# Mamba outer outputs in the inner outputs' bank, last states turned after the loop, and every low weight on VectorE

## The reference

```python
for l in range(2):
    h = h + 0.5 * swiglu(rms_norm(h, norm_ffn1[l]), ...)      # 1024 -> 2*2816 -> 1024
    u = rms_norm(h, norm_mix[l])
    m = mixer_ab(u) if l == 0 else mixer_c(u)                 # Mamba-2 + GLA, or HGRN2
    h = h + m
    h = h + 0.5 * swiglu(rms_norm(h, norm_ffn2[l]), ...)
y = rms_norm(h, norm_final)
```

```python
xdt = xb * dt
y = einsum(C B^T * decay, xdt)  +  (C h) * exp(cum)  +  D * x     # inner + outer + skip
h_new = h * exp(cum[-1]) + einsum(B, exp(cum[-1] - cum), xdt)      # the state, and at the end an output
y = rms_norm(y * silu(z))
```

## Time and profile before

| | us |
|---|---|
| median of 3 runs | 2534.32 (2531.28 to 2534.85) |
| the profiled execution | 2535.39 |
| its span | 2533.7 |
| TensorE busy | 2439.3 (96%) |
| VectorE, ScalarE, GpSimd busy | 1138.3, 988.4, 680.7 |
| mean granted TensorE clock | 0.984 of 2.4 GHz |

### The profile page before, as it was taken

The page is one execution under the profiler, slowest core; times in us unless marked ns, Lnnn a source line. Parts: engine busy times, 40 slices in busy tenths (PEclk is TensorE's granted clock), DMA queues, the critical chain, the costliest instruction groups (busy, mean ns, idle before and its releaser), DMA issues.

```text
span 2533.7 us, 53953 instructions
## 1 busy us (share of the span) xinstructions
PE 2439.3 (96%) x21434; PEld 2401.3 (95%) x21434; DVE 1138.3 (45%) x1730; ACT 988.4 (39%) x1416; POOL 680.7 (27%) x292
## 2 busy tenths in 40 slices
PE   7999999888899999999999999999999988999998
PEld 7999999887899999999999999999999987999998
DVE  3330335777566653321344330335788854330334
ACT  4331224556345444321223331223777734331222
POOL 3443443000000003443443443443000002443442
PEclk9999999899999999999999999999999998999999
DMA  4332233232322223232332232332222222232231
GB/s 120 89 103 74 83 97 83 70 97 68 99 81 64 67 74 87 83 108 68 90 99 75 84 108 67 91 95 80 64 65 71 62 64 64 87 104 74 84 96 56
DMA packets 395808, 208.80 MB, mean 82 GB/s; under 512 B 9791, under 2 KB 391862, under 8 KB 395670
## 3 DMA queue, kind: packets, MB, share of 16 engines
q1 hardware_dynamic: 390094, 203.09, 27.9%
q10 hardware_dynamic: 5576, 3.77, 0.5%
HBM read 201.39 MB, written 5.45 MB: 82 GB/s over the span
## 4 chain that ended last, share of the span: by engine, by line
PE 85%; DVE 7%; ACT 2%; DVEq 2%; issue 1%; ACTq 1%; POOL 0%; DMA 0%; SPq 0%; POOLq 0%
PE PD L1865 67%; PE PD L1892 12%; PE PM L2205 1%; DVE wlo L1137 1%; PE PM L2215 1%; DVE CV L1292 1%; ACTq L978 1%; PE PM L2238 1%; ACT whi L521 1%; DVEq L1610 1%; POOL wlo L466 0%; DVE c_xl L1608 0%; PE PM L2199 0%; PE PM L2183 0%; PE PM L2064 0%
## 5 line engine op out<-in xcount | busy, mean ns | idle before, releaser
L466 POOL TENSOR_TENSOR wlo<-raw,whi 128x1024 fp32r<-128x1024 f32 (+2 forms) x244 | 668.8, 2741 | 1551.3 <-ACT whi L521 1538.6
L521 ACT ACTIVATE whi<-raw 128x1024 fp32r<-128x1024 f32 (+4 forms) x348 | 381.5, 1096 | 1147.3 <-PE PD L1865 1025.8
L1865 PE MATMUL PD<-XH,whi 128*128 128x272 f32 x3008 | 624.4, 289 | 5.9 <-POOL wlo L466 2.9
L1865 PE MATMUL PD<-XH,wlo 128*128 128x272 f32 x3008 | 621.8, 288 | 0.0
L1865 PE MATMUL PD<-XL,whi 128*128 128x272 f32 x3008 | 621.3, 288 | 0.0
L1865 PEld LDWEIGHTS PD<-XH,whi 128*128 128x128 f32 x3008 | 473.1, 188 | 8.0 <-issue 4.0
L1865 PEld LDWEIGHTS PD<-XL,whi 128*128 128x128 f32 x3008 | 473.5, 189 | 0.0
L1865 PEld LDWEIGHTS PD<-XH,wlo 128*128 128x128 f32 x3008 | 470.8, 189 | 0.0
L1865 PE MATMUL PD<-AL,whi 128*128 128x272 f32 x1408 | 291.3, 288 | 0.0
L1865 PE MATMUL PD<-AH,whi 128*128 128x272 f32 x1408 | 291.1, 288 | 0.0
L1865 PE MATMUL PD<-AH,wlo 128*128 128x272 f32 x1408 | 290.2, 287 | 0.0
(11 more groups left out here) (402 smaller groups left out, 2616.7 us busy)
## 6 DMA issues: line engine op xcount, KB each, us to landing
raw<-in_ffn_w_gu SPq DMA_DIRECT2D x176, 512.0 KB, 3.8
raw<-in_ffn_w_down SPq DMA_DIRECT2D x32, 768.0 KB, 4.8
raw<-in_ab_w_in SPq DMA_DIRECT2D x44, 512.0 KB, 4.0
raw<-in_ffn_w_down SPq DMA_DIRECT2D x32, 640.0 KB, 4.5
raw<-in_c_w_in SPq DMA_DIRECT2D x32, 512.0 KB, 4.1
LM<-cum_rows SPq DMA_DIRECT2D x8, 512.0 KB, 4.9
raw<-in_ab_w_out SPq DMA_DIRECT2D x16, 256.0 KB, 2.8
raw<-in_ab_w_out SPq DMA_DIRECT2D x8, 512.0 KB, 4.0
```

The lines of the kernel that those rows point to most:

```text
L466: pool.tensor_tensor(wlo[u % 2][:, 0:k, :], raw[u % 4][:, 0:k, :], whi[u % 2][:, 0:k, :].bitcast(F), ALU.subtract).then_inc(S["lo_ready"], 1)
L521: A(whi[ps % 2][:, 0:k, :], raw[ps % 4][:, 0:k, :], ACT.Copy).then_inc(S["hi_ready"], 1)
L1865: last = mm(PD[:, 2 * (ps % 2) + s, 0:HT], wt[ps % 2][:, r, :], x[:, r, s * HT:(s + 1) * HT], start=(p == 0 and q == 0), stop=(p == 2 and ...
```

## The change

- **Outer outputs.** `outputs(j)` writes them to bank 1, columns 32 to 479, beside the 32 inner columns of the sample; `y_read` of pair j-1 is now waited for there, and `output(j)` on DVE reads them there. `turn(j)` waits for x alone.
- **Last states.** The chain of DVE leaves them untransposed in HIO and HSIO; PE turns all eight of a kind at once, into banks 2 and 3: `state_turn(0)` behind `outputs(7)`, `state_turn(1)` behind unit 6 of `ab_outy0`. ACT copies them back with two copies each. SS has two tiles less.
- **Means.** They go to banks 0 and 1. `mean(0)` stands ahead of `products(5)` instead of `turn(5)`, ACT's `y_rstd(0)` behind `decay(5)`, and `outputs(5)` waits for it. The wait for `y_read` of the last pair moves from ahead of unit 5 to behind the first half of unit 6, and the last rows' copy (CLST) behind `y_rstd(1)`.
- **DVE's order at m = 7.** The four `y_low` go ahead of `gate_row(7)`.
- **Low weights.** POOL makes units 0 and 1 only; DVE makes all others, each (`lo_ahead`) behind the evacuation of the unit two before it, inside the loops, which now go over four units with the last round written out.

```diff
@@ POOL
-            def lo(u, i, k):
...
+            for u in range(2):
+                pool.wait_ge(S["hi_ready"], u + 1)
+                pool.tensor_tensor(wlo[u][:, 0:KT, :], raw[u][:, 0:KT, :], whi[u][:, 0:KT, :].bitcast(F),
+                                   ALU.subtract).then_inc(S["lo_ready"], 1)
+            pool.wait_ge(S["unit_done"], plan["ab_heads"][0] + CREDIT)
+            states_out(pool)
+            scan_consts(GM)
+            pool.wait_ge(S["rs_ready"], 5)
+            scan_consts(CM)
@@ ACT
-            def state_rows(j):
-                act.wait_ge(S["st_turned"], j + 1)
-                A(HIO[:, j, :], PM[:, 1, P:2 * P], ACT.Copy)
-                A(HSIO[:, j, :], PM[:, 1, 2 * P:3 * P], ACT.Copy)
+            def state_rows(n):
+                act.wait_ge(S["st_turned"], n + 1)
+                for b in range(2):
+                    A((HIO, HSIO)[n][:, 4 * b:4 * b + 4, :], PM[:, 2 + b, :].rearrange("p (m q) -> p m q", m=4), ACT.Copy)
                 act.drain().then_inc(S["hout_copied"], 1)
@@ in spreads
                 if j == 0:
                     sample_decays()
-                else:
-                    state_rows(j - 1)
@@ in the steps
                 weights(ux + 2 * m + 3)
-                if m == 5:
-                    y_rstd(0)
                 gate_silus(m)
                 if m < KT - 1:
                     decay(m)
+                if m == 5:
+                    y_rstd(0)
@@ behind the loop
             weights(uy + 6)
-            act.wait_ge(S["last_psum"], 1)
-            state_rows(j)
-            A(CLST[:, :], PM[:, 1, 3 * P:4 * P], ACT.Copy).then_inc(S["last_copied"], 1)
+            state_rows(0)
             weights(uy + 7)
             weights(uy + 8)
             y_rstd(1)
+            A(CLST[:, :], PM[:, 1, P:2 * P], ACT.Copy).then_inc(S["last_copied"], 1)
             weights(uy + 9)
             for m in range(4, KT):
                 y_high(m)
+            state_rows(1)
@@ DVE
+            def lo_ahead(u0, b, i, k, last):
+                if last:
+                    u = u0 + 4 * i + b + 2
+                    if u < len(unit_rows):
+                        lo(u)
+                    return
+                u = u0 + b + 2
+                hold("dve", S["hi_ready"], 4 * i + (u + 1))
+                TT(wlo[u % 2][:, 0:k, :], raw[u % 4][:, 0:k, :],
+                   whi[u % 2][:, 0:k, :].bitcast(F), ALU.subtract).then_inc(S["lo_ready"], 1)
@@ DVE, up projection
+                    def body(i, last=False):
+                        for t in range(2):
+                            for b in range(2):
+                                hold("dve", S["unit_done"], 4 * i + (u0 + 2 * t + b + 1 + CREDIT))
+                                up(None, u0 + b, b)
+                                lo_ahead(u0, 2 * t + b, i, k, last)
+                            hold("dve", S["silu_done"], 2 * i + (base + t + 1))
...
+                    loop("dve", 0, n // 4 - 1, body)
+                    body(n // 4 - 1, True)
@@ DVE, output
-                TT(ep, PM[:, 2:4, :].rearrange("p s t -> p (s t)")[:, CH:T], ep, ALU.mult)
+                TT(ep, PM[:, 1, TS:TS + T - CH], ep, ALU.mult)
@@ DVE, behind the loop
-            gate_row(j)
             for n in range(4):
                 y_low(n)
+            gate_row(j)
@@ DVE, HGRN output projection
-                    if turn < 2:
+                    if turn < 3:
                         low(8, 7 + turn)
                     x_out(5, m, turn=turn)
+                low(8, 10)
@@ PE, turn(j)
                 pe.wait_ge(S["xc_ready"], 4 + j + 1)
-                if j >= 5:
-                    pe.wait_ge(S["y_rstd"], 1)
-                if j:
-                    pe.wait_ge(S["y_read"], j)
-                    state_turn(j - 1)
-                else:
+                if j == 0:
                     pe.wait_ge(S["cb_masked"], 1)
@@ PE, outputs(j)
+                if j:
+                    pe.wait_ge(S["y_read"], j)
+                if j == 5:
+                    pe.wait_ge(S["y_rstd"], 1)
                 for c in range(1, NC):
-                    mm(PM[:, 2, c * CH:(c + 1) * CH], SS[:, c - 1, :], cg[:, c * CH:(c + 1) * CH], start=True, stop=True)
...
-                if j:
-                    pe.wait_ge(S["hout_copied"], j)
+                    mm(PM[:, 1, TS + (c - 1) * CH:TS + c * CH], SS[:, c - 1, :], cg[:, c * CH:(c + 1) * CH], start=True, stop=True)
@@ PE, steps and end
                 x_rows(m, 0, 3)
+                turn(j)
+                x_rows(m, 3, 6)
                 if j == 5:
                     pe.wait_ge(S["y_read"], j)
                     mean(0)
-                turn(j)
-                x_rows(m, 3, 6)
                 products(j)
...
             outputs(j)
+            state_turn(0)
             out_rows(3, 2, 4)
             out_rows(4, 0, 4)
+            out_rows(5, 0, 4)
+            out_rows(6, 0, 2)
             pe.wait_ge(S["y_read"], KT)
             pe.wait_ge(S["last_rows"], 1)
-            state_turn(j)
-            pe.transpose(PM[:, 1, 3 * P:4 * P], XLAST[:, :], ident[:, :]).then_inc(S["last_psum"], 1)
-            out_rows(5, 0, 4)
-            out_rows(6, 0, 2)
+            pe.transpose(PM[:, 1, P:2 * P], XLAST[:, :], ident[:, :])
             mean(1)
             out_rows(6, 2, 4)
+            state_turn(1)
             out_rows(7, 0, 4)
```

More of the change, by code:

```diff
@@ L181, in build @@
         EP = place("EP", [T], w)
-        SS = place("SS", [NC + 1, P], w)
+        SS = place("SS", [NC - 1, P], w)
         DTT = place("DTT", [NC + 1, 48], w)
@@ L1252, in _ @@
             TSC(LB[:, 3, :], LB[:, 2, :], -1.0, 1.0, ALU.mult, ALU.add)
+            dve.wait_ge(S["lo_ready"], 2 + CREDIT)
             ffn("l0f1", 1)
@@ L1679, in out_lo @@
                         dve.drain().then_inc(S["head_out"], 1)
-                if not gla:
-                    dve.wait_ge(S["lo_ready"], u0 + 2 + CREDIT)
                 units(0, 0)
@@ L2039, in chunk_pairs, with state_turn @@
                 last.then_inc(S["cb_psum"], 1)
[L2041 to L2044 removed]
+            def state_turn(n):
+                if n:
+                    pe.wait_ge(S["hout_copied"], 1)
+                for m in range(KT):
+                    last = pe.transpose(PM[:, 2 + m // 4, (m % 4) * P:(m % 4 + 1) * P], (HIO, HSIO)[n][:, m, :], ident[:, :])
+                last.then_inc(S["st_turned"], 1)
             def turn(j):
                 pe.wait_ge(S["xc_ready"], 4 + j + 1)
[L2049 to L2054 removed]
+                if j == 0:
                     pe.wait_ge(S["cb_masked"], 1)
```

96 lines of the change are left out of this document (28 added, 68 removed).

## The result

The changed kernel takes 2517.95 us (median of five executions, 2513.09 to 2521.20) where the kernel before, beside it on the chip, took 2531.28 (2530.98 to 2534.85): a ratio of 0.994 with a 95% interval of 0.9923 to 0.9957. (The ratio compares the means of the executions; that of the medians is 0.9947.) It is faster, by 13.3 us between the medians where 9.7 were forecast. Five more executions in the experiments gave 2521.26 us in the median and a ratio of 0.9948 (0.9934 to 0.9962); over all ten the median is 2519.7 us, some 11.8 us less than before. The profiled execution took 2514.17 us (span 2512.2), one of the shorter ones, so its trace flatters the change by about 5 us.

A forecast was written before the change was run, and what follows sets the result against it. TensorE, busy for 2439.3 of 2533.7 us, was taken as the bound. Savings of 2.9, 1.2, 2.0, 0.9, 2.7, 1.5 and 0.25 less 1.8 added made 9.65 us, so a median of 2524.6 us; range 2517.5 to 2531.

The forecast's parts named there:

- rival 2: Mamba stage: fewer gaps keep the clock full in two or three further stretches, 1.7 us each; 2520 us; chance 0.16.
- Starts of the feed-forward stages: Four waits of TensorE on GpSimd's low weights at these starts go once VectorE makes them; 2.9 us saved.
- HGRN output projection: XL shortens by 1.65 us without GpSimd beside it, less some 0.45 for the low weight behind H; 1.2 us saved.
- The turn of x: Mamba step 2: the turn no longer waits for y_read, idle falls from 2.20 to about 1.0; 2.0 us saved, nothing later.
- State copies out of the steps: Mamba steps 3 and 4: ScalarE's two copies and TensorE's two transposes leave, 0.45 us each; 0.9 us saved (0 to 2).
- Step 5: Mamba stage: y_rstd(0) and mean(0) move later, products start 3.0 us earlier, outputs(5) slightly late; 2.7 us saved (1.2 to 3.0).
- y_low: End of the Mamba loop: the four start earlier, so TensorE's 7.64 us gap shrinks by 1.5 us.
- What is added: Out units: eight state transposes cost 1.8 us; 0.25 us comes back from two transposes leaving the last turn.
- Nothing that another engine does faster there is worth anything, except where TensorE waits: Feed-forward stages: TensorE is busy throughout at full clock, 0.125 us per matmul, so faster other engines gain nothing outside waits.
- a mean clock above 0.96: Sign in the Mamba stage that would show the more-clock case, against a mean of 0.94 before.
- Rival 1: Mamba steps 2 to 5 gain nothing because VectorE's order and EP's landing set the rhythm; 2530.3 us; chance 0.28.
- Rival 3: Seams from up to down projection: VectorE's queue becomes the bound; 2536.6 us at 1.5 us over per seam; chance 0.04.

The follow-up runs named there:

- turn_waits: The kernel after, but the turn of x waits again for VectorE's reading of the last outputs; 2518.72 us, ratio to before 0.995.
- before_again: The kernel before, unchanged, run and traced a second time; 2532.40 us against 2531.51 for its twin, ratio 1.0002.
- low_only: The kernel before with only the low weights moved from GpSimd to VectorE; 2526.89 us, ratio to before 0.9978.
- mamba_only: The kernel after with GpSimd making the feed-forward low weights as before, leaving only the Mamba part of the change; 2524.65 us, ratio to before 0.9971.
- the last kernel here: The kernel after with VectorE's inputs(0), inputs(1) ahead of taps, HGRN's H ahead of the previous column's XL and ACC, and gap-fitted filler matmuls; 2504.20 us, ratio 0.989.
- fill: The kernel after with matmuls that compute nothing put into TensorE's idle gaps, some running past the gaps' ends; 2518.14 us, ratio to before 0.9946.
- fill_fit: The kernel after with fewer matmuls that compute nothing, cut to fit TensorE's idle gaps; 2515.99 us, ratio to before 0.9939.
- after_again: The kernel after, unchanged, run and traced a second time; 2521.26 us, ratio to before 0.9948.

## Why the prediction was right, and where it was not

The direction held, and so did most of the mechanisms. The size did not: 9.65 us forecast, 13.3 in the first comparison, 11.8 over ten executions. That 2517.95 lies in the stated range (2517.5 to 2531) is luck: the range's lower end was said to be rival 2 with its third stretch, which is 2524.6 - 3 x 1.7 = 2519.5 us, and that leaves the first median outside and the 2519.7 of ten executions just inside. By the steps of the working:

- **Starts of the feed-forward stages**, 2.9 us: right mechanism, 3.8 measured. I took the idle time in the row of the wait (0.80); the stage was longer by 1.04 at a start.
- **HGRN output projection**, 1.2 us: 1.26. The shorter XL and the low weight behind H are there with the sizes worked out.
- **The turn of x**, 2.0 us at step 2 and nothing later: 1.4 from turn 1 to 3 by the second traces, of which 1.0 is the wait with the half clock behind it (`turn_waits`). The clock did not fall behind the shorter gap, as I had counted on. From step 3 on the edit gives nothing, as said.
- **State copies out of the steps**, 0.9 us: 0.8 between the two first traces, in which EP lands late (19.15 against 18.36), and nothing between the second ones. The period of 17.97 us in VectorE's queue hides them otherwise. The earlier trace rows showed a late DMA, and I took its wait for the kernel's.
- **Step 5**, 2.7 us: 3.6 from turn 4 to 6. I had the products 3.0 us earlier; counted from turn 4 they start at 21.8 us where `before_again` and `low_only` have 25.2, so 3.4 earlier. The 0.2 to 0.7 us of lateness at `outputs(5)` that I took off did not come, since RY was ready 0.9 us before it was wanted, and 0.2 more is gained up to the next turn. EP's issue did move with the turn, against what I wrote: it follows the taps, by 2.68 us in both traces.
- **y_low**, 1.5 us: the gap fell by 1.47, and 1.2 is left from turn 6 to YH.
- **What is added**, 1.8 less 0.25: the out part is 0.7 us longer by the second traces. It is 2.3 longer by the first.

These measured terms make 3.8 + 1.26 + 1.4 + 3.6 + 1.2 - 0.7 = 10.6 us, and 11.4 with a late EP.

**The step that failed** is the one that gave TensorE's own speed no term outside the named waits. It has two parts.

- *"Nothing that another engine does faster there is worth anything, except where TensorE waits"*, with 0.125 us per matmul throughout. In both traces of before the second and the third feed-forward stage take 399.1 us; in `mamba_only`, with the same waits, 398.0. So 2.2 us of the difference lie in stages where TensorE waits for nothing and PEclk is 1.00 in both kernels. None of the other fourteen traces has it there. Its cause is open. GpSimd's low weights alone do not bring it, since `mamba_only` has them. With these 2.2 us the terms make 12.8 us against the 11.8 over ten executions, which is within the scatter.
- *The clock*, which beyond the places of steps 2 and 5 stood in a rival as all or nothing (**rival 2**, 0.16, 2520 us). It was neither: behind step 5 the half clock went in every trace, behind step 2 in the three of four that had it. The first pair of traces shows 14.2 us of shorter matmuls, the second pair 5.2, so most of the first figure is luck of one trace. The rival's time is nearer to the result than the forecast's 2524.6, but its mechanism, two or three stretches on top, was not shown: `mamba_only` at 2524.65 us lies by the forecast's 2525.7 and not by the 2517 to 2520 of the clock theory, and the sign set for it, a mean clock above 0.96 from 434 to 724 us, reads 0.96.

The terms that were mis-sized most are the starts, step 5 and what is added, each too small by 0.9 us, and the state copies, too large by 0.9.

**Rival 1** (0.28) fell with the 4 to 6 distances. **Rival 3** did not show: no wait for AL or for a low weight in a feed-forward stage.

## What to carry over

Compare the distance between equal events of neighbouring steps, not the waits alone, and in two traces of the same kernel: a late DMA or a stretch at half clock in one of them looks like the cost of an instruction. Before an order is changed in one engine's queue, list what stands behind the moved instruction in every other queue that waits for it. Where TensorE sets the pace and idles for some microseconds, matmuls that compute nothing and are no longer than the gap gave 7 us in the last kernel here (and nothing that the time could resolve in `fill` and `fill_fit`); in the HGRN tail, where VectorE sets it, they gave none, and swapping two of its instructions took a column from 3.21 to 2.49 us.

## What the hardware showed that I had not expected

- **The clock differs between executions of one kernel.** Ten of after gave 2513.1 to 2523.0 us with mean granted clocks of 0.989 to 0.986, and the three fastest (2513.1, 2514.0, 2514.2) are the three at 0.989. The Trainium skill ("TensorE: Matmul & The Clock Gate", What's actually happening) says that the number of slow matmuls is run-variable, and the traces agree; it puts the penalty of the ramp at under 1% of a typical span, and here the scatter alone, 0.4%, is more than most single edits are worth.
- **Which gaps cost clock**: behind 3.59 us at step 5 it fell in 4 traces of 4, behind 2.20 us at step 2 in 3 of 4 (before twice and `turn_waits`; not in `low_only`), behind 2.48 us at step 4 the once that this gap was so long (first trace of before), behind the gaps of 1.0 to 2.1 us ahead of the turns of step 2 to 6 in none of the sixteen traces. These are counts at these places and no rule: what TensorE did ahead of the gap differs from place to place.
- **A float32 matmul of 128 by 128 is two records and 0.22 us** at full clock (16 of them in 3.57 us above), where a float32r matmul of 272 columns is one record and 0.125 us.
- **Full clock is not always quite full.** In both traces of before the second and third feed-forward stage took 399.1 us where the 396.96 of `low_only` and the 1.04 of the start make 398.0, with PEclk at 1.00 throughout: the stream ran 0.3% slow, 2.2 us in all. No kernel with either half of the change has it there; `before_again`, `low_only`, `after_again` and four more have the same pace (125.3 to 125.6 ns per matmul in place of 125.0) in the first stage. I have no cause for it.
- **EP's landing** differs by 1.4 us between two executions with the same issue, and moved the step behind it by 0.4 to 1.2 us. Landings about 0.9 us late (step 4 of `turn_waits` and of the first trace of after) moved nothing: these steps took 17.96 and 17.97 us.
